# The odd mixer's values take x's chunks in the order 1, 2, 3, 0, and VectorE turns chunk 0

## The chip, the cores and the metric

The kernel runs on one core of a Trainium2 chip. The metric is the device time of one execution in microseconds (us), lower is better; the time of a kernel is the median of several executions. Engines are named as in the profile: PE is TensorE (PEld its weight loads), DVE is VectorE, ACT is ScalarE, POOL is GpSimd, SP is SyncE, which only issues DMAs here.

## The reference

One sequence of 256 tokens, 2048 features, fp32, goes through two layers. Layer 0 has the even mixer, layer 1 the odd mixer; each mixer is followed by a feed-forward part, and both read a normalised x. The change touches the seam between the feed-forward part of layer 0 and the odd mixer:

```python
h = rms_norm(x, norm_mix_g[i])              # x * rsqrt(mean(x*x) + eps) * g
p = h @ w_in_odd[o]                         # 2048 -> q, k, v (2048 each), 16 forget gates
f_logit = (p[..., 3 * C_WIDTH:] + b_forget[o]).astype(jnp.float32)
log_f = jax.nn.log_sigmoid(f_logit)
c = jnp.cumsum(log_f, axis=1)               # over the tokens
logits = q @ k * scale + c[query] - c[key]  # 16 heads of 128, causal
probs = jax.nn.softmax(logits) ; att = probs @ v
x = x + att @ w_out_odd[o]
x = x + conv_ffn(rms_norm(x, norm_ffn_g[i]), w_up[i], conv_w[i], conv_b[i], w_down[i])
```

## The kernel before

**Pieces.** All weights stream once from HBM in pieces of 128 x 2048 fp32 (1 MB), through a ring of four slots. For each piece SP loads `w_raw`, ACT rounds it to `w_high` (function `high`), DVE writes the remainder `w_low = w_raw - w_high` (`low`), and PE multiplies. The activations are split in the same way: `H` (`h_split`) holds 16 blocks of 128 features, each with 256 columns of the high part and 256 of the low part. Each product is high x high, high x low and low x high. The whole order is written by hand: each engine has its own program, loops over pieces k, and waits on counting semaphores. ACT and DVE prepare piece k + 3 (`LEAD`) in step k. A piece is used either by `straight_quad` (tokens x 512 outputs, 4 feature blocks; lines 1374) or by `turned_half` (outputs x tokens, 8 feature blocks; lines 1335 and 1344).

**Turning x.** H wants x with features on partitions. x is 256 tokens x 2048 features, and is turned in four chunks of 512 features. `transpose_x(s, n)` does it on PE, eight 128 x 128 transposes into two banks of `ps_turned`. `turn_blocks(s, n, tokens)` does it on DVE in squares of 32 x 32, from x into `work`; its `tokens` name quarters of the rows, and four instructions turn one quarter. Then `turned_high` on ACT makes the high half of four blocks of H from the turned chunk, in two pairs, and `turned_low` on DVE the low half, each pair after ACT's. Here s is the normalisation (0 even mixer, 1 its feed-forward part, 2 odd mixer, 3 its feed-forward part). The rows of x are not yet scaled by the root mean square: its inverse (`rstd`) is made in the chain `squares` (ACT), `mean_square` (DVE), `root` (ACT), `spread_rstd` (DVE, writes `diag`), `spread` (PE, two small products with `diag`), `take_rstd` (DVE), and applied later.

**The seam.** The last sixteen pieces of layer 0's feed-forward part end with four `straight_quad`s (k = 12 to 15 of that loop), each adding 512 features to x (`add_to_x` on DVE, line 893). In the kernel before, `transpose_x(2, 0)` follows the quad k = 13 on PE, `transpose_x(2, 1)` follows k = 14, `transpose_x(2, 2)` follows k = 15, and `transpose_x(2, 3)` follows the first quad of the odd mixer. The odd mixer's first group (`heads_of_group(0)`) has four quads for the values v (k = 0 to 3), which use chunks 0, 1, 2, 3 of H in this order, and eight `turned_half`s for q and k of four heads. In between lie the forget gates: `forget_sums` (all 16 blocks of H times the gate weights, needs the whole of H; line 1654) after k = 1, `turn_forget_sums` (line 1665) after k = 2, an exponential and a logarithm on ACT, `cumulate` (lines 1675 to 1681) after k = 4, and then POOL stores the sums and reads them back spread over the partitions as `bias`, which the first head's logits (DVE line 1187) need behind PE's `scores` (line 1626).

Of the kernel before, what the change touches and what calls it, by code (L numbers as in the profile page):

```python
# [49 lines left out]
def build(nc, x_in, norm_mix_g, norm_ffn_g, final_norm_g, w_in_even, ln_v_g, ln_v_b, w_spatial,  # L50
# [23 lines left out]
    N_END = N_FFN[1] + 12 * NG  # L74
    OUT0_ORDER = [(c, q) for c in range(4) for q in (2, 3, 0, 1)]
    OUT1_ORDER = [(0, 0), (0, 1), (0, 2), (1, 0), (1, 1), (1, 2), (0, 3), (1, 3)] + \
                 [(c, q) for c in (2, 3) for q in range(4)]
# [23 lines left out]
    with ExitStack() as ctx:  # L101
# [64 lines left out]
        fl, fe, lf = (work[:, 5632 + 32 * i:5664 + 32 * i].rearrange("p (t h) -> p t h", t=2) for i in range(3))  # L166
        final_g = work[:, 0:2048]
        xT = [work[:, 1024 * i:1024 * i + 1024].rearrange("p (k t) -> p k t", k=4) for i in range(3)]
        scaled = raw[:, 0:2, :]
# [106 lines left out]
        def turned_bank(s, n, kk):  # L276


            if s in (1, 3) and n < 3:
                return xT[n][:, kk, :]  # L280
            ps, b = (psA, 0) if s in (1, 3) else (psT, 2 * (n % 2))
            return ps[:, b + kk // 2, TOK * (kk % 2):TOK * (kk % 2) + TOK]

        block = ctx.enter_context(nc.Block())
# [3 lines left out]
        def _(sp):  # L288
# [75 lines left out]
            def load_heads(r):  # L364

                first = N_MIX1 - 12
                col = value(sp, at(2 * D - 512, 512, r))
                for q in range(4):
                    load(first + q, W_IN1[:, 4 * q:4 * q + 4, bass.ds(col, 512)], r)
                for pair in range(2):  # L370
                    for j in range(2):
                        col = value(sp, at(256 * pair + D * j - 512, 512, r))
                        for k in range(2):
                            load(first + 4 + 4 * pair + 2 * j + k, W_IN1[:, 8 * k:8 * k + 8, bass.ds(col, 256)], r)
# [64 lines left out]
        def _(a):  # L439
# [47 lines left out]
            def turned_high(s, n):  # L487

                if s == 0 and n == 0:
                    a.wait_ge(s_turn_a, 1)  # L490
                else:
                    a.wait_ge(s_turn, 4 * s + n + 1)
                for kk in range(4):
                    k = 4 * n + kk
                    if s == 0 and n == 0 and kk == 2:
                        a.wait_ge(s_turn, 1)
                    ins = a.activation(H[:, k, 0:TOK], turned_bank(s, n, kk),
                                       ACT.Copy, scale=cols[:, GAIN[s] + k:GAIN[s] + k + 1])
                    if kk % 2:
                        fenced(ins, s_turn_hi, 8 * s + 2 * n + kk // 2 + 1)  # L500

# [132 lines left out]
            def ffn(l):  # L634
# [39 lines left out]
                for k in range(16):  # L674
                    if k >= 14 and l == 0:
                        turned_high(s + 1, k - 14)
                    high(c + k + LEAD)
# [51 lines left out]
            def heads_of_group(first, r=0):  # L729

                c = N_MIX1 + 12 * first
                for k in range(12):
                    hh = 4 * first
                    if first == 0 and k == 0:
# [3 lines left out]
                        root(2)  # L738
                    if first == 0 and k == 2:
                        a.wait_ge(s_f, 1)  # L740
                        fenced(a.activation(fT, psA[0:2 * HEADS, 2, :], ACT.Copy), s_fT, 1)
                    if first == 0 and k == 3:
                        a.wait_ge(s_fl, 1)
                        link(a.activation(fe, fe, ACT.Exp))
                        fenced(a.activation(fe, fe, ACT.Ln, bias=1.0), s_fe, 1)
# [76 lines left out]
        def _(ve):  # L822
# [37 lines left out]
            def turned_low(s, n):  # L860

                for kk in range(4):
                    k = 4 * n + kk
                    if kk % 2 == 0:
                        ve.wait_ge(s_turn_hi, 8 * s + 2 * n + kk // 2 + 1)
                    ins = ve.scalar_tensor_tensor(
# [3 lines left out]
                    if s == 0 and n == 0 and kk == 1:  # L870
                        ins.then_inc(s_turned_a, 1)
                        ve.wait_ge(s_raw_a, 16)
                        fenced(ve.tensor_copy(wh[:, 0, 0:PIECE // 2], raw[:, 0, 0:PIECE // 2]), s_high_a, 1)
                fenced(ins, s_turned, 4 * s + n + 1)

            def turn_blocks(s, n, tokens):


                for i in tokens:
                    for j in range(4):  # L880
                        src = x[32 * i:32 * i + 32, :, 512 * n:512 * n + 512]\
                            .rearrange("p t (k j b) -> p t k j b", k=4, j=4)[:, :, :, j, :]
                        dst = xT[n][32 * j:32 * j + 32, :, :].rearrange("p k (t i b) -> p t k i b", t=2, i=4)[:, :, :, i, :]
                        ins = ve.transpose(dst, src)  # L884
                if 3 in tokens:
                    ins.then_inc(s_turn, 1)
# [207 lines left out]
            def ffn(l):  # L1094
# [46 lines left out]
                for k in range(16):  # L1141
                    if k >= 14 and l == 0:
                        turned_low(s + 1, k - 14)
                    low(c + k + LEAD)
# [21 lines left out]
                    if k >= 8 and not (l == 1 and k >= 12):  # L1166
                        add_to_x(A_FFN[l] + 4 * (NG - 2) + k - 8, k % 4, c + k)

            ffn(0)


# [37 lines left out]
            def heads_of_group(first, r=0):  # L1209
                c, hh = N_MIX1 + 12 * first, 4 * first  # L1210
                for k in range(12):
                    if first == 0 and k == 0:
                        turned_low(2, 2)
                        turned_low(2, 3)
                        mean_square(2)
                        spread_rstd(2)
                    if first and k in (1, 3, 5):
                        head_low(hh - 3 + k // 2, psA[:, 3, :], r)
# [8 lines left out]
                    low(c + k + LEAD, r)  # L1227
                    if first == 0 and k == 1:
                        take_rstd(2)
                        link(ve.tensor_scalar(q_rstdT, rstdT[:, :], float(P) ** -0.5, None, ALU.mult))  # L1230
                    if first == 0 and k == 2:

                        ve.wait_ge(s_ft, 1)
                        for t in range(2):
# [3 lines left out]
                               s_fl, 1)  # L1238
                    if first == 0 and k == 3:
                        ve.wait_ge(s_fe, 1)  # L1240
                        fenced(ve.scalar_tensor_tensor(out=lf, in0=fl, scalar=0.0, in1=fe, op0=ALU.min, op1=ALU.subtract),
                               s_lf, 1)
                    if first == 0 and k == 4:
                        ve.wait_ge(s_c, 1)
# [68 lines left out]
        def _(pe):  # L1313
# [74 lines left out]
            def transpose_x(s, n):  # L1388

                if n < 2:  # L1390
                    if s:
# [3 lines left out]
                else:  # L1395
                    pe.wait_ge(s_turned, 4 * s + n - 1)
                if s:
# [152 lines left out]
            def down(l, g, c, r=0, frm=0, transposes=False):  # L1550
# [5 lines left out]
                for n in range(4):  # L1556
                    i = A_FFN[l] + 4 * g + n
                    pe.wait_ge(s_xadd, at(i - 1, 4, r))
                    straight_quad(c + n, n % 2, Y, 4 * frm, True, True, r)
                    if transposes and n >= 1:  # L1560
                        transpose_x(2, n - 1)
# [123 lines left out]
            def heads_of_group(first, r=0):  # L1685
                c, hh = N_MIX1 + 12 * first, 4 * first
                for k in range(12):
                    if k < 4:
# [4 lines left out]
                        elif k == 0:  # L1693
                            pe.wait_ge(s_vr, at(first, 1, r))
                        straight_quad(c + k, 0, H, 4 * k, k == 0, k == 3, r)
                    else:
# [8 lines left out]
                    if first == 0 and k == 0:  # L1705
                        transpose_x(2, 3)
                    if first == 0 and k == 1:
                        forget_sums()
                        spread(2)
                    if first == 0 and k == 2:  # L1710
                        turn_forget_sums()
                    if first == 0 and k == 4:
                        cumulate()
# [61 lines left out]
```

## Time and profile before

| | us |
|---|---|
| median of 3 runs (2101.19 to 2101.7) | 2101.42 |
| the profiled execution, its own time | 2101.76 |
| its span in the trace | 2100.0 |
| PE busy | 2087.7 (99%) |
| PEld busy | 1802.7 (86%) |
| DVE busy | 1493.8 (71%) |
| ACT busy | 1045.8 (50%) |
| granted TensorE clock | 0.999 of full |

The span is the stretch that the trace covers; the rest of the profiled execution's own time lies around it. Busy time is the time in which an engine has an instruction running. PE's share says that nearly the whole span is covered by matmuls one after another, so the time is PE's list of instructions plus the places where it waits.

### The profile page before, as it was taken

The numbers are of one execution on the slowest core, as the hardware profiler recorded it, in microseconds if no ns is written. First come the engines' busy times: TensorE is split into PE (matmuls) and PEld (weight loads), VectorE is DVE, ScalarE is ACT, GpSimd is POOL, SyncE is SP. The second block draws the span as 40 slices with busy tenths as digits, with TensorE's granted clock in tenths as the row PEclk, the third lists the DMA queues.
The fourth block names the chain that finished last, engine by engine and source line by source line (L and its number), as shares of the span: only waits on it lengthen the run. The fifth ranks groups of instructions, "written<-read, shape, count | busy, mean of one in ns | idle before, by whom it ended". The sixth has DMA issues, their size and how long they took to land.

```text
span 2100.0 us, 29629 instructions
## 1 busy us (share of the span) xinstructions
PE 2087.7 (99%) x11034; PEld 1802.7 (86%) x11034; DVE 1493.8 (71%) x1692; ACT 1045.8 (50%) x1078; POOL 30.2 (1%) x59
## 2 busy tenths in 40 slices
PE   9999999999999999999999999999999999999998
PEld 7888888888888888888888888888888888888886
DVE  6788786777667776776556655977776767767677
ACT  7554564445444454455444444554454444444454
POOL 0000000000000000000101000000000000000000
PEclk9999999999999999999999999999999999999999
DMA  8655565555555555564665555565655556555552
GB/s 300 198 172 196 168 216 192 190 196 186 187 198 182 200 180 190 196 196 154 197 187 175 186 176 187 171 207 184 200 180 188 193 181 209 188 180 198 181 194 106
DMA packets 317298, 397.16 MB, mean 189 GB/s; under 512 B 8724, under 2 KB 240956, under 8 KB 317116
## 3 DMA queue, kind: packets, MB, share of 16 engines
q1 hardware_dynamic: 313500, 391.27, 56.3%
q0 software_dynamic: 1056, 3.16, 0.7%
q10 hardware_dynamic: 2688, 1.99, 0.3%
q8 instruction: 36, 0.59, 0.1%
q14 instruction: 18, 0.15, 0.0%
HBM read 394.29 MB, written 2.11 MB: 189 GB/s over the span
## 4 chain that ended last, share of the span: by engine, by line
PE 99%; DMA 0%; DVE 0%; SPq 0%; ACT 0%; issue 0%; DVEq 0%; ACTq 0%
PE ps_turned L1335 39%; PE ps_straight L1374 36%; PE ps_turned L1344 20%; DMA x<-in_x 0%; PE ps_turned L1406 0%; PE ps_straight L1627 0%; PE ps_straight L1644 0%; PE ps_straight L1636 0%; PE ps_straight L1507 0%; PE ps_straight L1654 0%; PE ps_turned L1583 0%; PE ps_turned L1579 0%; PE ps_straight L1583 0%; PE ps_straight L1579 0%; PE ps_turned L1578 0%; PE ps_straight L1578 0%
## 5 line engine op out<-in xcount | busy, mean ns | idle before, releaser
L842 DVE TENSOR_TENSOR w_low<-w_raw,w_high 128x2048 fp32r<-128x2048 f32 x369 | 846.1, 2294 | 402.1 <-ACT w_high L459 364.2
L459 ACT ACTIVATE w_high<-w_raw 128x2048 fp32r<-128x2048 f32 x368 | 704.9, 1918 | 667.9 <-PE ps_straight L1374 293.2
L1335 PE MATMUL ps_turned<-h_split,w_high 128*128 128x512 f32 x3584 | 832.2, 390 | 0.0
L1335 PEld LDWEIGHTS ps_turned<-h_split,w_high 128*128 128x128 f32 x3584 | 667.6, 188 | 135.3
L1344 PEld LDWEIGHTS ps_turned<-h_split,w_low 128*128 128x128 f32 x3584 | 440.7, 192 | 6.1 <-issue 0.2
L1344 PE MATMUL ps_turned<-h_split,w_low 128*128 128x256 f32 x3584 | 445.3, 283 | 0.0
L1374 PE MATMUL ps_straight<-w_high,y_split 128*128 128x512 f32 x1856 | 440.5, 390 | 0.0
L1374 PEld LDWEIGHTS ps_straight<-w_high,y_split 128*128 128x128 f32 x1856 | 347.9, 188 | 72.0
L1374 PE MATMUL ps_straight<-w_low,y_split 128*128 128x512 f32 x928 | 229.2, 389 | 0.0
L1374 PEld LDWEIGHTS ps_straight<-w_low,y_split 128*128 128x128 f32 x928 | 174.2, 188 | 36.2
L1075 DVE SCALAR_TENSOR_TENSOR work<-work,conv_columns 128x256 f32<-128x256 f32 x352 | 154.6, 480 | 10.9
L893 DVE TENSOR_TENSOR x<-x,ps_straight 128x512 f32<-128x512 f32 x184 | 118.1, 683 | 55.3 <-PE ps_straight L1374 54.5
L617 ACT ACTIVATE work<-work,conv_columns 128x256 f32<-128x256 f32 x176 | 95.6, 591 | 65.1 <-DVE work L852 65.1
L468 ACT ACTIVATE work<-ps_turned 128x512 f32<-128x512 f32 x112 | 67.2, 600 | 109.2 <-PE ps_turned L1335 89.0
L848 DVE TENSOR_TENSOR work<-ps_turned,work 128x512 f32<-128x512 f32 x112 | 77.2, 690 | 19.3 <-ACT work L468 16.3
L1374 PE MATMUL ps_straight<-w_high,h_split 128*128 128x512 f32 x368 | 90.5, 398 | 0.0
L1374 PEld LDWEIGHTS ps_straight<-w_high,h_split 128*128 128x128 f32 x368 | 68.1, 188 | 14.2 <-issue 0.5
L852 DVE TENSOR_TENSOR work<-work,rstd_rows 128x512 f32<-128x512 f32 x103 | 71.8, 697 | 3.5
L1374 PE MATMUL ps_straight<-w_low,h_split 128*128 128x512 f32 x184 | 45.5, 389 | 0.0
L884 DVE STREAM_TRANSPOSE work<-x 32x256 f32<-32x256 f32 x96 | 41.8, 436 | 1.5
L1374 PEld LDWEIGHTS ps_straight<-w_low,h_split 128*128 128x128 f32 x184 | 34.5, 188 | 7.2
L1086 DVE TENSOR_TENSOR work<-work 128x512 f32<-128x512 f32 x44 | 30.5, 693 | 5.0
(204 smaller groups left out, 609.6 us busy)
## 6 DMA issues: line engine op xcount, KB each, us to landing
w_raw<-in_w_up SPq DMA_DIRECT2D x176, 1024.0 KB, 5.0
w_raw<-in_w_down SPq DMA_DIRECT2D x88, 1024.0 KB, 5.0
w_raw<-in_w_in_odd SPq DMA_DIRECT2D x48, 1024.0 KB, 5.3
w_raw<-in_w_in_even SPq DMA_DIRECT2D x23, 1024.0 KB, 5.4
w_raw<-in_w_out_even SPq DMA_DIRECT2D x16, 1024.0 KB, 5.0
w_raw<-in_w_out_odd SPq DMA_DIRECT2D x16, 1024.0 KB, 5.0
work<-c_rows POOLq DMA_DIRECT2D x8, 256.0 KB, 4.5
x<-in_x SPq DMA_DIRECT2D x3, 512.0 KB, 11.2
```

The lines of the kernel that those rows point to most:

```text
L459: a.activation(wh[:, s, :], raw[:, s, :], ACT.Copy).then_inc(s_high, 1)
L468: fenced(a.activation(spare, src, ACT.Copy), s_spare, at(q + 1, 4, r))
L617: ins = a.activation(cc[j % 2][:, m, :], up[:, m, 2:], ACT.Identity, scale=taps[:, l, 2, bass.ds(i, 1)], bias=taps[:, l, 3, bass.ds(i, 1)])
L842: ve.tensor_tensor(wl[:, s, :], raw[:, s, :], wh[:, s, :].bitcast(F32), ALU.subtract).then_inc(s_low, 1)
L848: fenced(ve.tensor_tensor(to, src, spare, ALU.add), s_added, at(q + 1, 4, r))
L852: return ve.tensor_tensor(ap, ap, factor.unsqueeze(1).to_broadcast([P, 2, TOK]), ALU.mult)
L884: ins = ve.transpose(dst, src)
L893: ins = ve.tensor_tensor(xc, xc, psA[:, 2 * (i % 2) + t, :], ALU.add)
L1075: ins = ve.scalar_tensor_tensor(out=c[:, m, :], in0=up[:, m, 2 - back:TOK + 2 - back], scalar=taps[:, l, 2 - back, bass.ds(i, 1)], in1=c[: ...
L1335: ins = pe.matmul(psT[:, 2 * slot + m, :], hi[:, kk, P * m:P * m + P], acts[:, K, :], start=(K == 0 and not narrow_ran), stop=(K == KC - 1 ...
L1344: ins = pe.matmul(psT[:, 2 * slot + m, TOK:], lo[:, kk, P * m:P * m + P], acts[:, K, 0:TOK], start=(K == 0 and opens), stop=(K == KC - 1), ...
L1374: return pe.matmul(psA[:, 2 * slot + t, :], acts[:, k0 + kk, a0:a0 + P], weights[:, kk, :], start=begin, stop=end)
```

## The change

Chunk 0 of x is no longer turned by PE but by DVE, a quarter at a time: the quarters 0, 1 and 2 in the steps k = 13, 14 and 15 of the last feed-forward loop, and quarter 3 in step k = 1 of the odd mixer, ahead of `take_rstd`. Its place in H is filled by ACT and DVE in step k = 2. The value quads take the chunks in the order 1, 2, 3, 0, and the semaphore counts of H follow (`place`). `forget_sums` moves from behind quad k = 1 to behind quad k = 3, `turn_forget_sums` from behind k = 2 to behind k = 4, `cumulate` from behind k = 4 to behind k = 6, with their partners on ACT and DVE. `spread(2)` stays behind quad k = 1. SP's loads of the values' weights follow the new order; their number and size are unchanged.

```diff
+    MIX1_ORDER = [1, 2, 3, 0]
+        xT0 = work[:, 2064:3088].rearrange("p (k t) -> p k t", k=4)
+            if s == 2 and n == 0:
+                return xT0[:, kk, :]
+        def place(s, n):
+            return 4 * s + (MIX1_ORDER.index(n) if s == 2 else n)
...
@@ SP, load_heads
-                for q in range(4):
-                    load(first + q, W_IN1[:, 4 * q:4 * q + 4, bass.ds(col, 512)], r)
+                for k, q in enumerate(MIX1_ORDER):
+                    load(first + k, W_IN1[:, 4 * q:4 * q + 4, bass.ds(col, 512)], r)
...
@@ ACT, last loop of ffn
-                    if k >= 14 and l == 0:
-                        turned_high(s + 1, k - 14)
+                    if k == 15 and l == 0:
+                        turned_high(2, 1)
@@ ACT, heads_of_group
                     if first == 0 and k == 2:
+                        turned_high(2, 0)
+                    if first == 0 and k == 4:
                         a.wait_ge(s_f, 1)
...
@@ DVE, last loop of ffn
-                    if k >= 14 and l == 0:
-                        turned_low(s + 1, k - 14)
+                    if k == 15 and l == 0:
+                        turned_low(2, 1)
...
+                    if l == 0 and k >= 13:
+                        turn_blocks(2, 0, (k - 13,))
@@ DVE, heads_of_group
+                    if first == 0 and k == 2:
+                        turned_low(2, 0)
...
                     if first == 0 and k == 1:
+                        turn_blocks(2, 0, (3,))
                         take_rstd(2)
...
@@ PE, last down of layer 0
-                    if transposes and n >= 1:
+                    if transposes and n >= 2:
                         transpose_x(2, n - 1)
@@ PE, heads_of_group
-                        straight_quad(c + k, 0, H, 4 * k, k == 0, k == 3, r)
+                        straight_quad(c + k, 0, H, 4 * MIX1_ORDER[k], k == 0, k == 3, r)
...
                     if first == 0 and k == 1:
+                        spread(2)
+                    if first == 0 and k == 3:
                         forget_sums()
-                        spread(2)
-                    if first == 0 and k == 2:
+                    if first == 0 and k == 4:
                         turn_forget_sums()
-                    if first == 0 and k == 4:
+                    if first == 0 and k == 6:
                         cumulate()
```

The next rows are PE's order before, from the value quad k = 1 to the value quad k = 2. Names are those of the program; what stands in brackets are the semaphores that a row waits for.

```order
L1374 MATMUL ps_straight<-w_low,h_split 128x512 x7
L1654 MATMUL ps_straight<-h_split,wf_split 32x512 [waits h_ready,forget_weights_split]
L1654 MATMUL ps_straight<-h_split,wf_split 32x512 x15
L1415 MATMUL ps_straight<-diag,ones 128x128 [waits diag_ready]
L1415 MATMUL ps_straight<-diag,ones 128x128
L1374 MATMUL ps_straight<-w_high,h_split 128x512 [waits high_ready,h_ready]
```

The same place in the changed kernel, up to the gate's products behind quad k = 3 (lines are numbered 15 higher there).

```order
L1389 MATMUL ps_straight<-w_low,h_split 128x512 x7
L1430 MATMUL ps_straight<-diag,ones 128x128 [waits diag_ready]
L1430 MATMUL ps_straight<-diag,ones 128x128
L1389 MATMUL ps_straight<-w_high,h_split 128x512 [waits high_ready,h_ready]
L1389 MATMUL ps_straight<-w_high,h_split 128x512 x15
L1389 MATMUL ps_straight<-w_low,h_split 128x512 [waits low_ready]
L1389 MATMUL ps_straight<-w_low,h_split 128x512 x7
L1389 MATMUL ps_straight<-w_high,h_split 128x512 [waits high_ready,h_ready]
L1389 MATMUL ps_straight<-w_high,h_split 128x512 x15
L1669 MATMUL ps_straight<-h_split,wf_split 32x512 [waits h_ready,forget_weights_split]
```

The sixteen gate products no longer stand between quad k = 1 and the wait for `diag`, nor between quad k = 1 and quad k = 3.

DVE's order before, from the writing of `diag` through steps k = 0, 1 and 2 of the odd mixer:

```order
L918 TENSOR_SCALAR diag<-ident,small 128x128
L842 TENSOR_TENSOR w_low<-w_raw,w_high 128x2048 [waits piece_used,high_ready,diag_ready]
L842 TENSOR_TENSOR w_low<-w_raw,w_high 128x2048 [waits piece_used,high_ready]
L924 COPY rstd_rows<-ps_straight 128x256 [waits rstd_spread]
L1230 TENSOR_SCALAR work<-rstd_rows 128x256 [waits rstd_ready]
L842 TENSOR_TENSOR w_low<-w_raw,w_high 128x2048 [waits piece_used,high_ready,vector_chain]
```

And in the changed kernel:

```order
L928 TENSOR_SCALAR diag<-ident,small 128x128
L852 TENSOR_TENSOR w_low<-w_raw,w_high 128x2048 [waits piece_used,high_ready,diag_ready]
L852 TENSOR_TENSOR w_low<-w_raw,w_high 128x2048 [waits piece_used,high_ready]
L894 STREAM_TRANSPOSE work<-x 32x2x4x32 x4
L934 COPY rstd_rows<-ps_straight 128x256 [waits rstd_spread]
L1245 TENSOR_SCALAR work<-rstd_rows 128x256 [waits rstd_ready]
L876 SCALAR_TENSOR_TENSOR h_split<-work,feature_columns,h_split 128x256 [waits turned_high,vector_chain]
L876 SCALAR_TENSOR_TENSOR h_split<-work,feature_columns,h_split 128x256
L876 SCALAR_TENSOR_TENSOR h_split<-work,feature_columns,h_split 128x256 [waits turned_high]
L876 SCALAR_TENSOR_TENSOR h_split<-work,feature_columns,h_split 128x256
L852 TENSOR_TENSOR w_low<-w_raw,w_high 128x2048 [waits piece_used,high_ready,h_ready]
```

The last quarter's four turns and the low half of chunk 0 stand behind the two `w_low` pieces that follow `diag`.

## Rows read from the trace of the kernel before

**Rows 1.** The page, part 1: busy us, share of the span, instructions.
```profile
PE 2087.7 (99%) x11034; PEld 1802.7 (86%) x11034; DVE 1493.8 (71%) x1692; ACT 1045.8 (50%) x1078; POOL 30.2 (1%) x59
```

**Rows 2.** Waits of PE, whole span: waiter, releaser, us, times, longest.
```profile
PE ps_straight L1422 <- POOL ones L395: 1.9, 1, 1.9
PE ps_straight L1438 <- DVE w_high L873: 1.9, 1, 1.9
```

**Rows 3.** Timeline of PE at the seam: start us, us, instruction, count.
```profile
956.38 3.79 PE L1374 MATMUL ps_straight<-w_high,y_split 128*128 128x512 f32 x16
...
961.82 1.04 PE L1406 MATMUL ps_turned<-ident,x 128*128 128x128 f32 x8
...
968.16 1.03 PE L1406 MATMUL ps_turned<-ident,x 128*128 128x128 f32 x8
...
980.83 1.03 PE L1406 MATMUL ps_turned<-ident,x 128*128 128x128 f32 x8
981.62 3.89 PE L1374 MATMUL ps_straight<-w_high,h_split 128*128 128x512 f32 x16
...
987.15 3.86 PE L1654 MATMUL ps_straight<-h_split,wf_split 128*32 128x512 f32 x16
990.86 0.60 PE L1415 MATMUL ps_straight<-diag,ones 128*128 128x128 f32 x4
991.22 3.89 PE L1374 MATMUL ps_straight<-w_high,h_split 128*128 128x512 f32 x16
...
996.85 1.06 PE L1665 MATMUL ps_straight<-small,work 32*128 32x16 f32 x8
997.84 3.92 PE L1374 MATMUL ps_straight<-w_high,h_split 128*128 128x512 f32 x16
```

**Rows 4.** Timeline of ACT at the seam; in brackets idle before, and releaser.
```profile
981.96 1.72 ACT L497 ACTIVATE h_split<-ps_turned,feature_columns 128x256 fp32r<-128x256 f32 x4 [3.10 <-PE ps_turned L1406]
```

**Rows 5.** Timeline of DVE at the seam.
```profile
976.57 1.68 DVE L866 SCALAR_TENSOR_TENSOR h_split<-ps_turned,feature_columns,h_split 128x256 fp32r<-128x256 f32 x4
982.90 1.68 DVE L866 SCALAR_TENSOR_TENSOR h_split<-ps_turned,feature_columns,h_split 128x256 fp32r<-128x256 f32 x4 [4.65 <-ACT h_split L497]
...
987.66 0.48 DVE L918 TENSOR_SCALAR diag<-ident,small 128x128 f32<-128x128 f32 x2
988.60 4.50 DVE L842 TENSOR_TENSOR w_low<-w_raw,w_high 128x2048 fp32r<-128x2048 f32 x2 [0.45 <-DVE diag L918]
993.01 0.42 DVE L924 COPY rstd_rows<-ps_straight 128x256 f32<-128x256 f32 x1
```

**Rows 6.** Timeline of DVE where it turns a chunk for s = 1.
```profile
185.58 3.59 DVE L884 STREAM_TRANSPOSE work<-x 32x256 f32<-32x256 f32 x8
```

**Rows 7.** Timeline of ACT right behind that turn.
```profile
189.21 1.86 ACT L497 ACTIVATE h_split<-work,feature_columns 128x256 fp32r<-128x256 f32 x4 [3.41 <-DVE work L884]
```

**Rows 8.** Timeline of PE from the gate's last product to the first head.
```profile
1010.06 0.38 PE L1681 MATMUL ps_straight<-work 128*16 128x128 f32 x2
...
1032.68 0.38 PE L1626 MATMUL ps_straight<-work 128*128 128x128 f32 x2
...
1038.91 0.49 PE L1636 MATMUL ps_straight<-ident,work 128*128 128x128 f32 x3
```

**Rows 9.** Timeline of POOL: the bias tile of the first heads.
```profile
1020.62 1.90 POOL L430 TENSOR_TENSOR work<-work,causal 128x256 f32<-128x256 f32 x2 [4.11 <-DMA work<-c_rows]
```

**Rows 10.** Timeline of DVE: the first head's logits and probabilities.
```profile
1033.54 0.74 DVE L1187 SCALAR_TENSOR_TENSOR work<-ps_straight,small,work 128x128 f32<-128x128 f32 x2 [1.26 <-PE ps_straight L1627]
...
1037.66 0.35 DVE L1199 TENSOR_SCALAR work<-work,small 128x256 f32<-128x256 f32 x1
```

**Rows 11.** Timeline of PE at the launch.
```profile
1.87 2.93 PE L1422 MATMUL ps_straight<-ones,ident 128*128 128x128 f32 x12 [1.87 <-POOL ones L395]
...
5.86 1.28 PE L1422 MATMUL ps_straight<-ones,ident 128*128 128x128 f32 x10
8.99 2.08 PE L1438 MATMUL ps_straight<-w_high,h_split 128*128 128x512 f32 x8 [1.85 <-DVE w_high L873]
```

More of the change, by code:

```diff
@@ L491, in turned_high @@
                 else:
-                    a.wait_ge(s_turn, 4 * s + n + 1)
+                    a.wait_ge(s_turn, place(s, n) + 1)
                 for kk in range(4):
@@ L499, in turned_high @@
                     if kk % 2:
-                        fenced(ins, s_turn_hi, 8 * s + 2 * n + kk // 2 + 1)
+                        fenced(ins, s_turn_hi, 2 * place(s, n) + kk // 2 + 1)
             def root(s):
@@ L739, in heads_of_group @@
                     if first == 0 and k == 2:
+                        turned_high(2, 0)
+                    if first == 0 and k == 4:
                         a.wait_ge(s_f, 1)
                         fenced(a.activation(fT, psA[0:2 * HEADS, 2, :], ACT.Copy), s_fT, 1)
-                    if first == 0 and k == 3:
+                    if first == 0 and k == 5:
                         a.wait_ge(s_fl, 1)
@@ L864, in turned_low @@
                     if kk % 2 == 0:
-                        ve.wait_ge(s_turn_hi, 8 * s + 2 * n + kk // 2 + 1)
+                        ve.wait_ge(s_turn_hi, 2 * place(s, n) + kk // 2 + 1)
                     ins = ve.scalar_tensor_tensor(
@@ L873, in turned_low @@
                         fenced(ve.tensor_copy(wh[:, 0, 0:PIECE // 2], raw[:, 0, 0:PIECE // 2]), s_high_a, 1)
-                fenced(ins, s_turned, 4 * s + n + 1)
+                fenced(ins, s_turned, place(s, n) + 1)
             def turn_blocks(s, n, tokens):
@@ L882, in turn_blocks @@
                             .rearrange("p t (k j b) -> p t k j b", k=4, j=4)[:, :, :, j, :]
-                        dst = xT[n][32 * j:32 * j + 32, :, :].rearrange("p k (t i b) -> p t k i b", t=2, i=4)[:, :, :, i, :]
+                        dst = (xT0 if s == 2 else xT[n])[32 * j:32 * j + 32, :, :].rearrange("p k (t i b) -> p t k i b", t=2, i=4)[:, :, :, i, :]
                         ins = ve.transpose(dst, src)
@@ L1238, in heads_of_group @@
                                s_fl, 1)
-                    if first == 0 and k == 3:
+                    if first == 0 and k == 5:
                         ve.wait_ge(s_fe, 1)
@@ L1388, in transpose_x @@
             def transpose_x(s, n):
-                if n < 2:
+                if n < 2 or s == 2 and n == 2:
                     if s:
@@ L1395, in transpose_x @@
                 else:
-                    pe.wait_ge(s_turned, 4 * s + n - 1)
+                    pe.wait_ge(s_turned, place(s, n - 2) + 1)
                 if s:
@@ L1707, in heads_of_group @@
                     if first == 0 and k == 1:
+                        spread(2)
+                    if first == 0 and k == 3:
                         forget_sums()
-                        spread(2)
-                    if first == 0 and k == 2:
+                    if first == 0 and k == 4:
                         turn_forget_sums()
-                    if first == 0 and k == 4:
+                    if first == 0 and k == 6:
                         cumulate()
```

## The prediction

> **What bounds the kernel now.** I read the page first. Its busy times put PE at 2087.7 of 2100.0 us [rows 1]; the other engines are far from full. PE's busy share counts overlapping instructions, so next I asked what PE waits for over the whole span: two waits, 1.9 us each, both in the first 9 us [rows 2]. Everything behind them is PE's own list, back to back. Two things follow. An instruction taken off PE's list is worth what it holds PE for, and every new wait of PE is paid in full, because nothing later has slack to take it back. ACT and DVE matter only through what PE would wait for. So the third view is the timeline of PE at the seam [rows 3], and beside it those of ACT and DVE [rows 4, 5].
>
> **What the change takes from PE.** Between two quads with nothing behind them PE needs 961.82 - 956.38 = 5.44 us; with a turn of one chunk in between it needs 968.16 - 961.82 = 6.34 us [rows 3]. So the eight transposes of chunk 0 are worth **0.90 us**. The row gives 1.03 for all eight with their tail, so they overlap each other.
>
> The Trainium skill (TensorE: Matmul & The Clock Gate, Part 4: PE-mode transpose) gives about 275 ns for one such transpose inside a kernel, for bf16. Taken eight times that would be 2.2 us and the kernel would end 1.3 us earlier than I say; the trace shows that the eight do not run one after another, and I keep to it.
>
> Everything PE does from there to the end of quad k = 1 thus comes 0.90 earlier, if its inputs are there. They are: the last feed-forward steps give DVE three quarters of a turn. A turn of half a chunk is 3.59 us for eight instructions [rows 6], a quarter 1.79. The first two quarters fall where DVE no longer fills chunk 0 (1.68 us in one go, a row like those of [rows 5]) and in its waits for PE. The third stands directly ahead of chunk 2's low half, which started at 976.57 without a wait before it: now about 976.57 - 0.90 + 1.79 + 0.2 = 977.7, done at 979.4. The quad k = 1, which uses it, starts at 981.62 - 0.90 = 980.72 [rows 3]. That cover is 1.3 us; if it were gone PE would wait by the excess.
>
> **First new wait: diag.** The gate's sixteen products held PE from 987.15 to 990.86, 3.71 us, and `spread` followed at 990.86 [rows 3]. Meanwhile DVE made `diag`, done at 987.66 + 0.48 = 988.14 [rows 5]. The gate's products were the cover of this chain. In the changed order they stand behind k = 3, `spread` directly behind quad k = 1, at 987.15 - 0.90 = 986.25. The chain to `diag` hangs on the turn of chunk 3: ACT waited for PE there [rows 4] and DVE for ACT [rows 5], so it moves by the same 0.90, to 987.24. With 0.1 for the semaphore, PE waits **1.1 us**, starts `spread` at 987.3, quad k = 2 0.36 later (991.22 - 990.86) at 987.7, and ends it 5.44 later at 993.1.
>
> **Second new wait: chunk 0.** Quad k = 3 needs chunk 0 of H, complete. DVE's order is `diag`, two `w_low` pieces, the last quarter's turns, and only then can ACT and DVE fill H. Step by step:
> - the two pieces start at 988.60 - 0.90 = 987.70. What follows them came 4.41 later (993.01 - 988.60) [rows 5]: 992.11;
> - the last quarter, 1.79 [rows 6]: 993.90;
> - ACT began 0.04 behind such a turn (185.58 + 3.59 = 189.17, start 189.21) and took 1.86 for its four blocks read from `work` [rows 6, 7]: 995.80. Its own queue is free: one `w_high` behind `root` and another stand before it, which DVE's two pieces wait for anyway;
> - DVE ended its low half 0.90 behind ACT's end (982.90 + 1.68 = 984.58 against 981.96 + 1.72 = 983.68) [rows 4, 5]: 996.70. `take_rstd` and the next operation, which stand between, fit while ACT works;
> - 0.1 for the semaphore: PE starts quad k = 3 at **996.8**.
>
> PE was free at 993.1, so it waits another **3.6 us**. The first wait lies inside this one: even without it, k = 3 could not start before 996.8.
>
> **The sum.** Before, quad k = 3 started at 997.84 with the gate's products and their turning already done [rows 3]. Now it starts at 996.8, 1.04 earlier, but has the gate's products still ahead (3.71) and the turning of their sums, 997.84 - 996.85 = 0.99, and 0.19 that PE lost around it (996.85 - 991.22 = 5.63 for a quad of 5.44). Sum: -1.04 + 3.71 + 0.99 + 0.19 = **+3.85 us**. By its parts: -0.90 + 1.1 + 3.6 = +3.8, the same. The span would be 2103.9 and the profiled execution 2101.76 + 3.9 = 2105.7. That execution was 0.34 above the median of 2101.42, so the median should be **2105.3**.
>
> **What I cost at nothing.** Quarters 0 to 2 on DVE, as above. `w_low` of step k = 2 comes about 4 us later than before, since chunk 0 and the turn stand ahead, but its piece is used three steps, over 16 us, later. The loads follow `w_low`, and each has the same three steps. The number of gate instructions is the same. ACT's `high` in step k = 4 is now queued behind the wait for the gate's sums, and is used three steps on as well.
>
> The gate's last product moves two halves later, and behind it is a chain with POOL. Before, from the end of `cumulate` (1010.06 + 0.38 = 1010.44) PE had four halves, 22.24 us or 5.56 each, until `scores` at 1032.68 [rows 8]; DVE took the logits 0.86 later [rows 10]. The bias tile was ready at 1020.62 + 1.90 = 1022.52 [rows 9], 12.1 behind `cumulate`. Now two halves are left: DVE could take the logits 11.12 + 0.86 = 12.0 behind `cumulate`. The slack of 11 us shrinks to nothing, -0.1. PE waits for it only at the turning of the probabilities, 1038.91 [rows 8], which DVE had ready at 1037.66 + 0.35 = 1038.01 [rows 10]. 0.8 us of cover remain: no cost, but thin.
>
> **The rivals.**
> - *Chunk 0 is in time* (0.06). Quad k = 3 would find H ready, because the last quarter slips in earlier, or because PE's list gives more time than I read. Then at most -0.90 from the transposes, 2100.5; with only the wait for `diag`, +0.2, 2101.6. Against it: DVE's queue is in order, and the two pieces stand ahead. For it only the 4.65 us that DVE idles at 978 [rows 5], which the order does not use.
> - *The clock falls* (0.12): the one that ends on the other side, slower by more than 0.2%. PE never pauses after the launch in the kernel before. Two pauses come now, the second of 3.6 us, and if PE's clock drops from 2.4 to 1.2 GHz in it, the quad behind it begins at half pace. At the launch twelve small products took 2.93 us where ten took 1.28 later [rows 11]; at the later pace the twelve would take 1.54, so that stretch lost 1.4. The pause of 1.85 before 8.99 cost nothing visible: eight wide products in 2.08, where sixteen take 3.89 [rows 3, 11]. It decides from a pause longer than that; no row tells where. Price +1.4, up to 5.4 if a whole quad went at half pace. Time: 2106.7.
> - *The bias tile comes late* (0.08). Its reads share the DMA engines with the weights. PE pays only what exceeds the cover of 0.8. If the tile came 1.8 us later than its row says, 1.0 more: 2106.3.
> - *My forecast, +3.9* (0.70), own range 3.4 to 4.4: without the semaphores' 0.1 and the 0.19 it would be 3.6, and 0.2 to 0.3 for matmuls starting on an empty array on top.
> - Something else, such as DVE's third quarter delaying quad k = 1 too (0.04): above +3.9 only by little, since it comes off the second wait unless it moves the chain to `diag`.
>
> The skill speaks against the change at the clock: the Trainium skill (TensorE: Matmul & The Clock Gate, HAM oscillation — how this bites in real kernels) says that TensorE waiting between bursts falls back to half rate and pays to come back. By that rule the second rival is what happens. This trace has no such pause, and the one at 7 us went without.
>
> **How the numbers follow.** The predicted time is that of the forecast, 2105.3. The range reaches up over the two slower rivals, and down to +2.6, which is the forecast if one of the steps to 996.8 overlaps with the next by 1.3 us: 2104.0 to 2106.9. Chunk 0 in time lies outside.
>
> 0.2% of 2101.4 is 4.2 us, about what a measurement of this kernel can tell from no change. The forecast's +3.9 is just inside. Of its 0.70 I put 0.17 above 4.2; both slower rivals are above (0.20, less 0.03 where the bias costs little), and 0.01 of the rest. That is 0.35 slower. Nothing forecast here gives 4.2 faster: 0.01. The remaining 0.64 is no change.
>
> **What would show it.** In the changed kernel's trace, PE should have two new waits at the seam: about 1.1 us at `spread`, released by DVE's `diag`, and 3.6 at the first product of quad k = 3, released by DVE's filling of chunk 0. The transposes on PE between 960 and 985 should be 24, not 32. Chunk 1's turn should start at 967.3, quad k = 3 at 996.8, `scores` at 1036.3. If the last quarter's turns stand before the two pieces in time, or quad k = 3 is gapless, the main step is wrong. If the quad behind the pause takes over 6 us, the clock fell. If POOL's tile ends over 0.9 us behind `scores`, the third rival has a share.

## The result, and the profile after

| | before | changed |
|---|---|---|
| median, us | 2101.39 (2101.19 to 2101.7) | 2108.58 (2107.53 to 2109.24) |
| span of the profiled execution | 2100.0 | 2107.4 |
| its own time | 2101.76 | 2109.24 |
| mean granted clock | 0.999 | 0.997 |

The ratio is 1.0033, 95% interval 1.0024 to 1.0042: 7.2 us slower, beyond the forecast of +3.9 and outside the range (2104.0 to 2106.9). The executions of the changed kernel also lie 1.7 us apart, those of before 0.5, and the profiled one is the slowest of its seven, 0.66 above the median.

I looked first at what PE waits for, over the whole span of the changed kernel (waiter, releaser, us in total, times, longest), against [rows 2]:

```profile
PE ps_straight L1389 <- DVE h_split L876: 3.4, 1, 3.4
PE ps_straight L1437 <- POOL ones L403: 1.9, 1, 1.9
PE ps_straight L1453 <- DVE w_high L883: 1.9, 1, 1.9
PE ps_straight L1430 <- DVE diag L928: 0.9, 1, 0.9
```

Both forecast waits are there, 0.9 at `spread` (forecast 1.1) and 3.4 at chunk 0 (forecast 3.6). They sum to 4.3, less 0.9 for the transposes, which leaves 3.4 of 7.2. So half of the loss must lie where PE does not wait. The timeline of PE at the seam, against [rows 3]; all of it stands 0.15 later than before because of the launch (this quad began at 956.38 before, at 956.53 now):

```profile
956.53 3.79 PE L1389 MATMUL ps_straight<-w_high,y_split 128*128 128x512 f32 x16
...
967.41 1.04 PE L1421 MATMUL ps_turned<-ident,x 128*128 128x128 f32 x8
...
980.88 3.89 PE L1389 MATMUL ps_straight<-w_high,h_split 128*128 128x512 f32 x16
...
987.44 0.71 PE L1430 MATMUL ps_straight<-diag,ones 128*128 128x128 f32 x4 [0.87 <-DVE diag L928]
987.91 3.89 PE L1389 MATMUL ps_straight<-w_high,h_split 128*128 128x512 f32 x16
991.63 1.98 PE L1389 MATMUL ps_straight<-w_low,h_split 128*128 128x512 f32 x8
997.01 6.53 PE L1389 MATMUL ps_straight<-w_high,h_split 128*128 128x512 f32 x16 [3.41 <-DVE h_split L876]
1003.38 1.97 PE L1389 MATMUL ps_straight<-w_low,h_split 128*128 128x512 f32 x8
1005.19 3.86 PE L1669 MATMUL ps_straight<-h_split,wf_split 128*32 128x512 f32 x16
```

Quad k = 3 starts at 997.01, 996.86 without the launch's 0.15 (forecast 996.8). But it takes 1005.19 - 997.01 = 8.18 us, where a quad takes 5.44. Its sixteen products with `w_high` run for 6.53, not 3.9, and the eight with `w_low` behind them at the usual 1.97. The view by windows says why (stretch, its length, PE busy with the number of instructions, granted clock, DMA share, GB/s):

```profile
990.00:995.00 5.00, 3.61 (x16) 1.00 0.71 227
995.00:996.00 1.00, 0.00 (x0) 0.90 1.10 350
996.00:997.00 1.00, 0.00 (x0) 0.50 1.09 347
997.00:998.00 1.00, 0.98 (x2) 0.50 0.80 253
...
1002.00:1003.00 1.00, 1.00 (x5) 0.69 0.78 217
1003.00:1004.00 1.00, 1.00 (x6) 1.00 1.07 379
```

The granted clock falls from 1.00 to 0.50 (from 2.4 to 1.2 GHz) at 995.8: the stretch from 995 to 996 has 0.90, so a fifth of it is at 0.50. PE's last product had ended 2.2 us earlier, at 991.63 + 1.98 = 993.61. The clock comes back at about 1002.6, 5.6 us after PE began to work again. This is the second rival of the prediction: the clock falls.

The two waits themselves came about step by step as forecast. DVE in the changed kernel, against [rows 5]:

```profile
975.95 1.78 DVE L894 STREAM_TRANSPOSE work<-x 32x256 f32<-32x256 f32 x4
977.75 1.66 DVE L876 SCALAR_TENSOR_TENSOR h_split<-ps_turned,feature_columns,h_split 128x256 fp32r<-128x256 f32 x4
982.16 1.68 DVE L876 SCALAR_TENSOR_TENSOR h_split<-ps_turned,feature_columns,h_split 128x256 fp32r<-128x256 f32 x4 [2.75 <-ACT h_split L505]
...
986.91 0.48 DVE L928 TENSOR_SCALAR diag<-ident,small 128x128 f32<-128x128 f32 x2
987.85 4.49 DVE L852 TENSOR_TENSOR w_low<-w_raw,w_high 128x2048 fp32r<-128x2048 f32 x2 [0.46 <-DVE diag L928]
992.37 1.80 DVE L894 STREAM_TRANSPOSE work<-x 32x256 f32<-32x256 f32 x4
...
995.21 1.75 DVE L876 SCALAR_TENSOR_TENSOR h_split<-work,feature_columns,h_split 128x256 fp32r<-128x256 f32 x4 [0.26 <-ACT h_split L505]
```

The last quarter is turned from 992.37 on and chunk 0 is complete at 995.21 + 1.75 = 996.96, while DVE stood idle for 2.75 us ahead of 982.16.

Before [rows 10] DVE took the first head's logits as soon as PE had the scores. Now it waits for POOL's tile:

```profile
1040.32 0.74 DVE L1199 SCALAR_TENSOR_TENSOR work<-ps_straight,small,work 128x128 f32<-128x128 f32 x2 [1.40 <-POOL work L438]
...
1044.31 0.35 DVE L1211 TENSOR_SCALAR work<-work,small 128x256 f32<-128x256 f32 x1
```

DVE has the probabilities ready at 1044.31 + 0.35 = 1044.66. PE, whose rows are these, comes for them 0.9 later and does not wait:

```profile
1039.33 0.38 PE L1641 MATMUL ps_straight<-work 128*128 128x128 f32 x2
...
1045.56 0.49 PE L1651 MATMUL ps_straight<-ident,work 128*128 128x128 f32 x3
```

`scores` stands at 1039.33 against 1032.68 in [rows 8], +6.65. PE's last group is 6.65 later too. The remaining 0.75 of the span's 7.4 lies behind the last instruction, which issues the store of the result: from there to the end of the span it is 4.8 us here and 4.0 before. The same 4.8 stands in the traces of e3 and e6 below, 4.0 in the other seven; why is not known, and it is no part of the seam. (The spans of all executions of the changed kernel are 2105.7 to 2107.4.)

### The profile page after: what moved, and what is told of

Its sections match the earlier page's. It is cut to its first block, busy times and chain, and to the rows that moved or that the text cites. A ratio compares the mean times of both kernels' runs of the same rounds, so it can differ in the third digit from the quotient of the medians.

```text
span 2107.4 us, 29626 instructions
## 1 busy us (share of the span) xinstructions
PE 2090.2 (99%) x11026; PEld 1804.1 (86%) x11026; DVE 1500.4 (71%) x1708; ACT 1045.8 (50%) x1078; POOL 30.1 (1%) x59
## 4 chain that ended last, share of the span: by engine, by line
PE 98%; DVE 0%; DMA 0%; ACT 0%; issue 0%; SPq 0%; DVEq 0%; ACTq 0%
PE ps_turned L1350 39%; PE ps_straight L1389 36%; PE ps_turned L1359 20%; DMA w_raw<-in_w_in_even 0%; PE ps_straight L1642 0%; PE ps_straight L1659 0%; PE ps_turned L1421 0%; PE ps_straight L1651 0%; PE ps_straight L1453 0%; PE ps_straight L1522 0%; PE ps_straight L1669 0%; PE ps_turned L1598 0%; PE ps_turned L1593 0%; PE ps_straight L1598 0%; PE ps_straight L1593 0%
## 5 line engine op out<-in xcount | busy, mean ns | idle before, releaser
L894 DVE STREAM_TRANSPOSE work<-x 32x256 f32<-32x256 f32 x112 | 48.8, 436 | 1.8
```

## The experiments

Each was run 5 to 11 times beside the kernel before on the same chip. Differences are between medians; the kernel before had 2101.69 us beside e1 to e4 and 2101.62 beside e5 to e8. The changed kernel stands at +7.2. One thing to keep in mind for the small waits: the trace counts a wait from the end of PE's last product, which where nothing is waited for overlaps the next one by 0.2 us, so a wait costs somewhat more than it shows.

| | us | against before | ratio, 95% | waits of PE at the seam | quad k = 3 |
|---|---|---|---|---|---|
| changed kernel | 2108.58 | +7.2 | 1.0033 [1.0024, 1.0042] | 0.9 and 3.4 | 8.18 |
| e1_quarter_early | 2101.78 | +0.1 | 1.0001 [0.9992, 1.001] | 0.9 | 5.44 |
| e2_spread_later | 2100.59 | -1.1 | 0.9995 [0.9986, 1.0004] | none | 5.57 |
| e3_fill_pause | 2106.34 | +4.65 | 1.0023 [1.0014, 1.0032] | 0.9 and 0.7 | 5.61 |
| e4_gate_only | 2102.77 | +1.1 | 1.0005 [0.9996, 1.0014] | 0.9 | 5.44 |
| e5_half_quarter | 2105.85 | +4.2 | 1.0019 [1.001, 1.0028] | 0.9 and 2.5 | 7.21 |
| e6_after_spread_later | 2108.59 | +7.0 | 1.0033 [1.0021, 1.0045] | 4.6 | 8.43 |
| e7_fill_late | 2103.27 | +1.65 | 1.0009 [1.0, 1.0018] | 0.9 and 1.2 | 5.58 |
| e8_turn_twice | 2109.47 | +7.85 | 1.0038 [1.0024, 1.0052] | 0.9 and 5.2 | 7.77 |

The last column runs from the quad's start to the start of the gate's products behind it. The waits and this column are of one profiled execution each.

### e1: the last quarter is turned earlier

```diff
@@ DVE, heads_of_group, step k = 0
                         turned_low(2, 2)
+                        turn_blocks(2, 0, (3,))
                         turned_low(2, 3)
@@ DVE, heads_of_group, behind step k = 1
-                        turn_blocks(2, 0, (3,))
@@ DVE and ACT: chunk 0 of H in step 1
-                    if first == 0 and k == 2:
+                    if first == 0 and k == 1:
                         turned_low(2, 0)
@@ a semaphore of its own for chunk 0
-                    ins.then_inc(s_turn, 1)
+                    ins.then_inc(s_turn0 if s == 2 else s_turn, 1)
...
```

> The changed kernel, but DVE turns the last quarter of chunk 0 in step k = 0 of the odd mixer, between the low halves of chunks 2 and 3, where it idled 2.75 us, and ACT and DVE fill chunk 0 of H in step k = 1 instead of k = 2 (a semaphore of its own for chunk 0). My theory: the loss is the wait for chunk 0 (3.4 us) with the clock's fall that it brings (the quad behind it took 8.18 us instead of 5.44); without the pause both go, quad k = 3 starts right behind k = 2, only the 0.9 us at spread stays and the eight transposes give 0.9 back: 2101.4, between 2101.1 and 2101.9, granted clock 1.00 throughout. Rival A, that the loss comes from DVE's sixteen turns or the new order of the chunks as such: still over 2104. Rival B, that the pause at spread alone lets the clock fall: a wait of 0.9 and a slow quad behind it, about 2104.

2101.78 us, inside the range of my theory. PE's timeline:

```profile
986.74 0.71 PE L1434 MATMUL ps_straight<-diag,ones 128*128 128x128 f32 x4 [0.87 <-DVE diag L932]
987.21 3.92 PE L1393 MATMUL ps_straight<-w_high,h_split 128*128 128x512 f32 x16
990.97 1.98 PE L1393 MATMUL ps_straight<-w_low,h_split 128*128 128x512 f32 x8
992.78 3.79 PE L1393 MATMUL ps_straight<-w_high,h_split 128*128 128x512 f32 x16
```

and DVE's, where the turn stands in what had been idle time:

```profile
978.74 1.79 DVE L898 STREAM_TRANSPOSE work<-x 32x256 f32<-32x256 f32 x4
981.39 1.75 DVE L880 SCALAR_TENSOR_TENSOR h_split<-ps_turned,feature_columns,h_split 128x256 fp32r<-128x256 f32 x4 [0.86 <-ACT h_split L509]
...
989.35 1.67 DVE L880 SCALAR_TENSOR_TENSOR h_split<-work,feature_columns,h_split 128x256 fp32r<-128x256 f32 x4
```

The same sixteen turns on DVE, the same order of the chunks and the same place of the gate: only the pause at quad k = 3 is gone, and with it 7.1 us. Rival A falls, and so does rival B: the wait of 0.87 stands there alone, and the quads behind it keep their pace. The 0.9 us of transposes saved and the wait for `diag` nearly cancel.

### e2: and spread behind quad k = 2

```diff
-                    if first == 0 and k == 1:
+                    if first == 0 and k == 2:
                         spread(2)
```

> As e1_quarter_early, and spread stands behind quad k = 2 instead of k = 1 on PE, so that quad k = 2 covers the chain to diag. My theory: no wait of PE at the seam, and the eight transposes are all that is left: 0.9 under before, 2100.5 (2100.2 to 2100.9). Rival: DVE now holds at take_rstd until PE's spread and its next low piece comes late, or the transposes' 0.9 is not real because they overlap the quads: 2101.4 or more.

2100.59 us. PE has no wait left at the seam; `spread` starts right behind the quad:

```profile
989.61 1.98 PE L1393 MATMUL ps_straight<-w_low,h_split 128*128 128x512 f32 x8
991.43 0.60 PE L1434 MATMUL ps_straight<-diag,ones 128*128 128x128 f32 x4
991.79 3.92 PE L1393 MATMUL ps_straight<-w_high,h_split 128*128 128x512 f32 x16
```

All eleven times (2100.31 to 2100.78) lie below all 33 of before (2101.16 to 2102.14), but the interval of the ratio (0.9986 to 1.0004) still holds 1, so by that measure the gain is not shown. The trace does show it at the seam: from the start of the feed-forward quad k = 13 to `scores` PE takes 1031.50 - 956.10 = 75.40 us, and 1032.68 - 956.38 = 76.30 before, which is the 0.90 of the transposes. It is the version that does what the change set out to do, and was the fastest of all that I ran.

### e3: PE works through the pause

```diff
+                            if k == 3:
+                                for _ in range(12):
+                                    pe.matmul(psT[:, 0, 0:P], ident[:, :], ones[:, :], start=True, stop=True)
                             pe.wait_ge(s_turned, 8 + k + 1)
```

> The changed kernel, with twelve small products (128 x 128 of constants, into a free bank, read by nobody) on PE ahead of its wait for chunk 0: PE works 2.9 of the 3.4 us in which it paused. My theory: the array doesn't pause, the clock stays at 2.4 GHz and quad k = 3 takes 5.4 to 5.5 us; the wait itself is paid as before, so about 2.7 less than the changed kernel: 2105.8 (2105.2 to 2106.1). Rival A, that the quad is slow for another reason (its operands, or DVE and ACT at the same memory): still 8.2 us, 2108.6. Rival B, the constants don't hold the clock up: 2108 to 2109.

2106.34 us, 0.2 above the range that I gave and 2.2 below the changed kernel; against before, +4.65 instead of +7.2, so 2.5 less. PE's timeline (the twelve products are 24 rows, as the two of `spread` are four):

```profile
993.21 2.84 PE L1707 MATMUL ps_turned<-ones,ident 128*128 128x128 f32 x24
996.74 3.96 PE L1389 MATMUL ps_straight<-w_high,h_split 128*128 128x512 f32 x16 [0.69 <-DVE h_split L876]
```

and its windows (the columns are those of the windows above):

```profile
996.00:997.00 1.00, 0.31 (x2) 1.00 1.11 351
997.00:998.00 1.00, 1.00 (x5) 1.00 0.58 181
```

The quad starts when it did (996.74 against 997.01; the launch accounts for the difference) and takes 5.61 us, up to the gate's products at 1002.35, with the clock at 1.00. The chunk is as late as in the changed kernel; work that computes nothing holds the clock. Both rivals fall. The clock's share of the loss is 8.18 - 5.61 = 2.6 us. What is left at the seam is 1036.49 - 956.24 - 76.30 = 3.95 us (from the feed-forward quad k = 13 to `scores`, as under e2), which is the forecast's +3.85. The rest of the +4.65 lies behind the last instruction, 4.8 us instead of 4.0.

### e4: only the gate moves

The edit puts only the gate's part of the change (`forget_sums` behind k = 3, its turning behind k = 4, `cumulate` behind k = 6, and their partners on ACT and DVE) into the kernel before.

> The kernel before, with only the forget gate moved two pieces later on PE, ACT and DVE (spread stays behind quad k = 1); PE turns all four chunks, in the old order. My theory: the gate's sixteen products covered the chain to diag; PE waits 0.9 to 1.1 at spread and nowhere else, the clock stays: 2102.3 (2102.0 to 2102.7). Rival: the bias tile, whose slack shrinks from 11 us to nothing, makes PE wait at the first probabilities: 2103 or more. Rival: moving the gate costs nothing: 2101.4.

2102.77 us, +1.1 against the kernel before beside it. One row is new:

```profile
988.15 0.71 PE L1415 MATMUL ps_straight<-diag,ones 128*128 128x128 f32 x4 [0.88 <-DVE diag L918]
```

The gate's products covered the chain to `diag`. Uncovering it makes PE wait 0.9 us and costs 1.1: from the feed-forward quad k = 13 to `scores` it is 1033.77 - 956.33 = 77.44 us, 1.14 more than before. The interval of the ratio (0.9996 to 1.0014) holds 1, so it is the trace and not the time that speaks against the second rival, that the move costs nothing. The first, a wait for the bias tile, would show as another wait of PE; there is none behind the launch.

### e5: a shorter pause

```diff
-                    for j in range(4):
+                    for j in range(2 if (s, tokens) == (2, (3,)) else 4):
```

> The changed kernel with two of the four turns of the last quarter left out (a part of chunk 0 keeps old values), so that chunk 0 is ready 0.9 us earlier and PE pauses about 2.5 instead of 3.4 us. The wait alone would then give 2101.4 + 3.9 + 0.2 - 0.9 = 2104.6 to 2105.4. My theory: the clock's fall depends on the length of the pause; in the changed kernel's trace it came 2.3 us into the pause, so here it falls just before the quad or not at all, and the cost lies anywhere between 0 and the 2.7 of the changed kernel: 2104.6 to 2107.7, with a spread over its executions. Rival: the fall belongs to the pause as such, or to the two pauses together, and costs 2.7 again: 2107.3 to 2107.9 with the granted clock down for nearly 7 us as before.

This version leaves out half of the last quarter's turns, so its result is not that of the model; it serves for its times alone. 2105.85 us, with its executions from 2104.17 to 2106.57, the widest of all. The profiled one is the slowest. Its pause is 2.5 us. PE's row and the windows:

```profile
996.18 5.54 PE L1389 MATMUL ps_straight<-w_high,h_split 128*128 128x512 f32 x16 [2.50 <-DVE h_split L876]
```

```profile
995.00:996.00 1.00, 0.00 (x0) 1.00 1.11 356
996.00:997.00 1.00, 0.82 (x4) 1.00 1.10 348
997.00:998.00 1.00, 1.00 (x4) 0.53 0.98 309
...
1000.00:1001.00 1.00, 1.00 (x5) 0.76 0.33 47
```

The clock held through the pause and fell 0.9 us after PE was back at work, 3.4 us after its last product ahead of the pause. It stayed down for 3.4 us, not for nearly 7 as the rival had it. The quad took 7.21, so 1.6 us went to the clock. I had the cost between 0 and 2.7 right, but not the moment: I thought that a fall not reached in the pause would not come. The three lowest executions, at +2.5 to +3.1, have a mean granted clock of 0.999, as before; the other eight have 0.998. That fits executions in which the clock did not fall at the seam at all, which no trace here shows.

### e6: one pause instead of two

The edit of e2, made to the changed kernel.

> The changed kernel with spread behind quad k = 2 instead of k = 1 on PE, nothing else. The wait of 0.9 at spread goes, PE comes to quad k = 3 earlier and waits there longer (4.3 instead of 3.4 us), since chunk 0 is ready at the same time. My theory: the first wait lies inside the second: same time as the changed kernel, 2108.6 (2107.5 to 2109.4). Rival A, the two waits add: 0.9 less, 2107.7. Rival B, the clock fell because there were two pauses close together: with one pause it stays and the time is 2105.8.

2108.59 us, the time of the changed kernel:

```profile
996.34 6.78 PE L1389 MATMUL ps_straight<-w_high,h_split 128*128 128x512 f32 x16 [4.55 <-DVE h_split L876]
```

The wait at `spread` is gone and the one at chunk 0 is 1.1 longer. So the first wait cost nothing beside the second, and the clock falls with a single pause too.

### e7: the quarter early, the filling late

e1 without its move of the filling to step 1.

> As e1_quarter_early (last quarter turned in step k = 0), but chunk 0 of H is filled in step k = 2 as in the changed kernel, behind the second low piece on DVE. My theory: quad k = 3 waits only for that piece: about 0.6 us more than e1_quarter_early, 2102.3 (2101.9 to 2102.8), and the clock stays in a pause so short. Rival: DVE's two low pieces are the main delay and not the turns: then quad k = 3 waits over 2 us and the time is 2104 or more.

2103.27 us, 0.5 above my range. PE waits 1.15 us at quad k = 3, not 0.6. I had forgotten that `take_rstd` and the operation behind it also stand ahead of the filling; DVE's rows give 0.78 for them:

```profile
992.06 0.42 DVE L938 COPY rstd_rows<-ps_straight 128x256 f32<-128x256 f32 x1
992.51 0.29 DVE L1249 TENSOR_SCALAR work<-rstd_rows 128x256 f32<-128x256 f32 x1
992.84 1.67 DVE L880 SCALAR_TENSOR_TENSOR h_split<-work,feature_columns,h_split 128x256 fp32r<-128x256 f32 x4
```

The quad behind the 1.15 took 5.58 and the granted clock stayed at 1.00: a pause this short left the clock alone. Against e1 the late filling costs 1.5 us, so the place of the turns, and not DVE's two pieces, was the main delay.

### e8: a longer pause

```diff
+                        turn_blocks(2, 0, (2,))
                         turn_blocks(2, 0, (3,))
```

> The changed kernel with four more turns in front of the last quarter's (quarter 2 once more, same values), which delays chunk 0 by 1.8 us: PE pauses 5.2 instead of 3.4 us. My theory: the longer wait is paid in full and the fall costs as before, since the clock comes back by work and not by waiting: 2108.6 + 1.8 = 2110.4 (2109.4 to 2111.2). Rival: the cost of the fall grows with the pause (a whole slow stretch more): 2111.5 or more.

2109.47 us, at the lower edge of my range and 0.7 above the changed kernel, not 1.8. The pause:

```profile
998.50 6.11 PE L1390 MATMUL ps_straight<-w_high,h_split 128*128 128x512 f32 x16 [5.19 <-DVE h_split L876]
```

```profile
996.00:997.00 1.00, 0.00 (x0) 0.68 1.10 356
...
1003.00:1004.00 1.00, 1.00 (x6) 0.91 0.63 122
```

It is 1.8 us longer, paid in full, and the quad takes 7.77 instead of 8.18. So the longer pause did not bring a dearer fall, but a slightly cheaper one. The windows show why. Read as above, the clock was at 0.50 from 996.4 to 1003.2, for 6.8 us, and 2.1 of them lay in the pause, where they cost nothing. In the changed kernel it was also 6.8 us (995.8 to 1002.6), but only 1.2 lay in the pause. What a fall costs is about half of the slow stretch in which PE works, from the quad's start, or from the fall where that comes later, until the clock is back:

| | PE's last product ends | clock falls | quad starts | clock is back | half of the slow work | measured (quad less 5.61) |
|---|---|---|---|---|---|---|
| e5_half_quarter | 993.7 | 997.1 | 996.2 | 1000.5 | 1.7 | 1.6 |
| e8_turn_twice | 993.3 | 996.4 | 998.5 | 1003.2 | 2.3 | 2.2 |
| changed kernel | 993.6 | 995.8 | 997.0 | 1002.6 | 2.8 | 2.6 |
| e6_after_spread_later | 991.8 | 995.7 | 996.3 | 1002.5 | 3.1 | 2.8 |

## Why the prediction was wrong

- **The transposes, -0.90.** Right: e2, where nothing else is left, is 0.90 shorter at the seam and 1.1 under before in its median.
- **First wait, for `diag`, 1.1.** Right: 0.87 in the trace, which leaves out the 0.2 of overlap; e4 shows it alone (+1.1). That it lies inside the second is shown by e6.
- **Second wait, for chunk 0, 3.6.** 3.41, and the quad started within 0.1 of the forecast. e1 removes it.
- **The sum, +3.85.** The waits, the transposes and the moved products are right: `scores` came +6.65, less 0.15 from the launch and 2.6 for the clock leaves +3.9, and e3 shows +3.95 there with the clock held. (The 1036.3 forecast for `scores` does not follow from this sum, which gives 1032.68 + 3.85 = 1036.5.) The time was another 0.75 longer in the profiled execution, behind the last instruction; for this the prediction had no term, and its cause stays open.
- **The clock. This step failed:** "*The clock falls* (0.12)", with "Price +1.4". It fell, and it cost 2.6 us, where the forecast had nothing. The failure was in what I took as evidence. The pause of 1.85 us at the launch [rows 11] cost nothing, and I stretched that to 3.6 us, although I had written that no row tells where it turns. The launch row told of pauses up to 1.85 and of nothing longer. And there was a row. Behind its last product the kernel before stands idle too, and its clock falls (PE's last group, then the windows with the columns of above):

```profile
2090.51 1.07 PE L1583 MATMUL ps_turned<-w_low,y_split 128*128 128x512 f32 x4
```

```profile
2093.00:2094.00 1.00, 0.00 (x0) 0.88 0.00 0
2094.00:2095.00 1.00, 0.00 (x0) 0.50 0.00 0
```

PE ended at 2091.58 and the clock fell at about 2093.8, 2.2 us later. A pause forecast at 3.6 was longer than that, so the trace that I had gave the rival more weight than 0.12. (At the ends of the other nine traces the clock fell 2.6 to 4.0 us after PE's last product.) The price was too low as well: +1.4 is what the first twelve products at the launch lost in 2.9 us, but a quad behind a pause has 5.4 us of work to be slowed. I had named that as the upper end (5.4) and left it out of the range. With 2.6 on top of the forecast the time would have been 2107.9; the remaining 0.7 is about what lies behind the last instruction.

- **The rule.** The prediction weighed a rule of the Trainium skill (TensorE: Matmul & The Clock Gate, HAM oscillation — how this bites in real kernels), that TensorE waiting between bursts falls back to half rate and pays to come back, and followed the launch row against it. The trace agrees with the rule: the clock was at 0.50 behind the pause, and the quad took 2.6 us more. The pause of 1.85 us in [rows 11] was not against it, only too short to bear on it.
- **The bias tile, 0.8 of cover.** Right: DVE got it 0.13 later than it could have used it (1040.32 against 1039.33 + 0.86), and PE had 0.9 to spare.
- **Work costed at nothing** (quarters 0 to 2, the later `w_low`, loads): right as far as the time goes. PE has no other wait at the seam in the changed kernel, and e1 and e2, which have the quarters and the loads, show no cost of them.

## What to carry to other kernels

Where TensorE is otherwise never idle, a wait of a few microseconds is not priced by its length alone: look whether the clock survives it, and carry the slow stretch behind it as a term of its own. The trace that you already have may tell how long the clock holds: look at the end of the kernel too, where the engine stops. Before moving work off such an engine, ask what that work was covering; here sixteen products of the gate hid a chain of small operations, and a turn placed behind two long operations in an in-order queue cost 7 us, while 2.75 us of idle time in the same queue stood a few rows earlier. If a pause can't be avoided, products that compute nothing can save the clock's part, 2.6 us here.

## What the runs showed of the hardware

- A pause of TensorE of 0.9 or 1.15 us left the granted clock at 1.00. Pauses of 2.5, 3.4, 4.6 and 5.2 us brought it to 0.50, each in the one execution that was profiled; at 2.5 us three other executions, with a mean clock of 0.999, look as if it had not fallen.
- The fall need not come in the pause. Behind the one of 2.5 us it came 0.9 us after work had resumed. Counted from PE's last product it came after 2.2 us (changed kernel, and the end of the kernel before), 3.0 (e8), 3.4 (e5) and 3.9 (e6), and after 2.6 to 4.0 at the ends of the other nine traces.
- A fall cost 1.6 to 2.8 us: about half of the slow stretch that fell on work. It did not grow with the pause, since what lies in the pause costs nothing: 0.7 us of 6.8 in e6, 1.2 of 6.8 in the changed kernel, 2.1 of 6.8 in e8, none of 3.4 in e5.
- Twelve 128 x 128 products of constants in 2.84 us held the clock at 1.00 across a wait of which only 0.7 us was left.
